# A hybrid decoder step on one core: sample values as one matmul per page on four column groups, and all convolution blocks as fused taps on VectorE

## What is computed

```python
u = glu_a * jax.nn.sigmoid(glu_g)
c, conv_new = causal_dwconv(u, conv_prev, conv_w, conv_b)      # 31 taps, 512 channels
...                                                            # LayerNorm over channels, SiLU -> a_out
z = jnp.einsum('bqhd,bkhd->bhqk', q, k) * (SB_HEAD_DIM ** -0.5) + bias
lb = jnp.where(mask, jax.nn.log_sigmoid(-z), 0.0)
rev = lax.cumsum(lb, axis=3, reverse=True)                     # 'after' is rev without its own key
wgt = jnp.where(mask, jnp.exp(jax.nn.log_sigmoid(z) + after), 0.0)
o = jnp.einsum('bhqk,bkhd->bqhd', wgt, v)
mixed = jnp.concatenate([a_out, o], axis=-1)
return mixed @ w_out, ...
```

## Time and profile before

| | us |
|---|---|
| median of 3 runs | 2577.05 (2575.78 to 2579.82) |
| the profiled execution | 2576.77 |
| its span in the trace | 2575.0 |
| VectorE busy in the span | 1362.9 (53%) |
| TensorE busy in the span | 2396.8 (93%) |
| GpSimd busy in the span | 426.9 (17%) |
| head loop, first to last subtraction of L1350 | 580.25 to 739.27 |
| output projection resumes | 772.58 |

### The profile page before, as it was taken

One profiled execution on the slowest core, in us unless ns is written; L12 is line 12 of the kernel. 1 busy time (PEld: TensorE's weight loads), 2 busy tenths in 40 slices (PEclk: granted clock), 3 DMA queues, 4 the chain that ended last, 5 costly groups with the idle time before them and its releaser, 6 DMA issues.

```text
span 2575.0 us, 45894 instructions
## 1 busy us (share of the span) xinstructions
PE 2396.8 (93%) x19221; PEld 2296.1 (89%) x19221; DVE 1362.9 (53%) x1492; ACT 826.5 (32%) x1025; POOL 426.9 (17%) x326
## 2 busy tenths in 40 slices
PE   7999999977989999999999998988889777999998
PEld 7999999864669999999999998878788767999997
DVE  4443444777834443445443444777676767443343
ACT  4221223134422221223221223352535343222223
POOL 0000012863303000003000002051423255000000
PEclk8999999977999999999999998989989898999999
DMA  4323226552422323223323323233232322333322
GB/s 134 92 80 106 81 82 179 172 167 81 141 65 66 88 79 110 82 74 107 98 81 99 98 68 102 67 97 88 74 94 83 103 62 78 85 86 102 98 74 75
DMA packets 409612, 244.48 MB, mean 95 GB/s; under 512 B 11363, under 2 KB 386475, under 8 KB 409441
## 3 DMA queue, kind: packets, MB, share of 16 engines
q1 hardware_dynamic: 409047, 242.61, 33.3%
q10 hardware_dynamic: 444, 0.17, 0.0%
HBM read 228.81 MB, written 14.58 MB: 95 GB/s over the span
## 4 chain that ended last, share of the span: by engine, by line
PE 76%; DVE 12%; ACT 5%; POOL 4%; issue 2%; DMA 0%; SPq 0%; ACTq 0%; POOLq 0%; DVEq 0%
PE PS L220 67%; POOL prod L872 3%; PE PS L1076 2%; DVE xcs L2028 2%; DVE cbuf L1251 1%; PE PS L959 1%; DVE wl L197 1%; PE PS L1810 1%; PE PS L1038 1%; DVE xcs L2195 1%; ACT wh L193 1%; DVE cdec L2206 1%; PE PS L1020 1%; PE PS L1727 1%; PE PS L969 1%
## 5 line engine op out<-in xcount | busy, mean ns | idle before, releaser
L220 PE MATMUL PS<-hh,wh 128*128 128x260 f32 x3792 | 776.5, 286 | 26.5 <-DVEq L637 7.6
L220 PE MATMUL PS<-hh,wl 128*128 128x260 f32 x3792 | 769.5, 285 | 0.0
L220 PE MATMUL PS<-hl,wh 128*128 128x260 f32 x3792 | 768.9, 285 | 0.0
L220 PEld LDWEIGHTS PS<-hh,wh 128*128 128x128 f32 x3792 | 590.6, 190 | 39.1 <-issue 22.5
L220 PEld LDWEIGHTS PS<-hh,wl 128*128 128x128 f32 x3792 | 589.2, 190 | 0.4
L220 PEld LDWEIGHTS PS<-hl,wh 128*128 128x128 f32 x3792 | 588.8, 190 | 0.4
L197 DVE TENSOR_TENSOR wl<-raw,wh 128x2048 fp32r<-128x2048 f32 (+2 forms) x194 | 442.7, 2282 | 205.3 <-ACT wh L193 204.8
L193 ACT ACTIVATE wh<-raw 128x2048 fp32r<-128x2048 f32 (+2 forms) x194 | 352.7, 1818 | 319.4 <-PE PS L220 283.9
L220 PE MATMUL PS<-hid_l,wh 128*128 128x260 f32 x1408 | 283.8, 283 | 0.0
L220 PE MATMUL PS<-hid_h,wh 128*128 128x260 f32 x1408 | 283.2, 282 | 0.0
L220 PE MATMUL PS<-hid_h,wl 128*128 128x260 f32 x1408 | 283.0, 282 | 0.0
(11 more groups left out here) (302 smaller groups left out, 2545.2 us busy)
## 6 DMA issues: line engine op xcount, KB each, us to landing
raw<-in_ffn_gate_dram SPq DMA_DIRECT2D x88, 512.0 KB, 4.0
raw<-in_ffn_up_dram SPq DMA_DIRECT2D x88, 512.0 KB, 5.2
raw<-in_ffn_down_dram SPq DMA_DIRECT2D x64, 384.0 KB, 4.1
raw<-in_ffn_down_dram SPq DMA_DIRECT2D x64, 320.0 KB, 3.6
raw<-in_m_in_proj_dram SPq DMA_DIRECT2D x40, 512.0 KB, 5.3
page<-in_cache_sb_v_dram SPq DMA_DIRECT2D x48, 256.0 KB, 2.7
raw<-in_ab_in_proj_dram SPq DMA_DIRECT2D x20, 512.0 KB, 5.3
ms_b<-in_state_ssm_dram SPq DMA_DIRECT2D x32, 256.0 KB, 3.0
```

Of the source, the lines that this page charges most:

```text
L220: ins = pe.matmul(out, x[:, k0, c:c + m], y[:, k, half * H2:(half + 1) * H2], start=k == 0 and a == 0, stop=k == nk - 1 and a == 2)
```

## The change

Three things are changed, all in `stage_a`.

1. **All four blocks on VectorE.** `tap`, GpSimd's additions and their semaphores go. `conv` runs over 124 taps instead of 93, 16 in a turn instead of 12.
2. **A page is one matmul.** The weights of all eight heads (8 columns of `dz`) stand in the array and the page's 512 columns stream past; the result is 8 rows by 512 columns, of which head h's row is wanted in its own 64 columns alone. Pages are taken in a new order (`value_page`): four samples at once, page pg of each, sample j of the four to the column group from row 32*j. `VROUNDS` becomes groups of four, at parts 1, 5 and 8 of turns 3, 4, 6, 7 and at parts 1 and 5 of turns 5 and 8; none is left in turn 9.
3. **The rows leave another way.** After four samples ScalarE copies the whole bank (`rows_out`, 128x512, twice in all) into `qb`, and at the end sixteen small matmuls against columns of `ident` pick each head's row out and turn it. The DMAs to `qrow` go. Bank 7 is zeroed once by VectorE (`orow_zero`), since these matmuls read all 128 rows; the first pages wait for it.

```diff
@@ on all engines
+                VQ = 4
+                two, three = ([0, VQ, 0, 0, 0, VQ, 0, 0, last] for last in (0, VQ))
+                VROUNDS = [0] * 3 * NR + (three * 2 + two) * 2 + [0] * NR
-                VROUNDS = [0] * 3 * NR + ([1] * (NR - 1) + [2]) * 6 + [1, 1, 0, 0, 0, 0, 0, 1, 1]
+                def value_page(v):
+                    g, r = divmod(v, VQ * NPG)
+                    pg, j = divmod(r, VQ)
+                    return g, pg, j
@@ on_sp
-                        load_page("cache_sb_v", i, vplace[i % NV], val_in[i % NV])
+                        g, pg, j = value_page(i)
+                        load_page("cache_sb_v", (g * VQ + j) * NPG + pg, vplace[i % NV], val_in[i % NV])
...
-                    for b in range(B):
-                        q = 32 * (b % 3)
-                        sp.wait_ge(S["orow_cp"], b + 1)
-                        sp.dma_start(qrow[b:b + 1, :], orow[b // 3][q:q + 1, :]).then_inc(S["orow_in"], 16)
@@ on_pool
-                    acc = cbuf[:, LC, 0:T]
-                    for w in range(1, CW):
...
-                        pool.tensor_tensor(acc, acc, prod[:, w % 2, :], ALU.add).then_inc(S["tap_add"], 1)
@@ on_pe, values()
+                            pe.wait_ge(S["orow_zero"], 1)
-                            if pg == 0 and b >= 3:
-                                pe.wait_ge(S["orow_cp"], b - 2)
-                            for h in range(NH):
-                                ins = pe.matmul(PS[q:q + 1, 7, h * DH:(h + 1) * DH], dz[:, b, pg, h:h + 1],
-                                                vplace[v % NV][:, h * DH:(h + 1) * DH], start=pg == 0 and h == 0,
-                                                stop=pg == NPG - 1 and h == NH - 1)
-                            ins.then_inc(S["dpv_mm"], 1)
+                            if pg == 0 and j == 0 and g >= 1:
+                                pe.wait_ge(S["orow_cp"], g)
+                            pe.matmul(PS[32 * j:32 * j + NH, 7, :], dz[:, g * VQ + j, pg, :], vplace[v % NV],
+                                      start=pg == 0, stop=pg == NPG - 1).then_inc(S["dpv_mm"], 1)
@@ on_pe, after the loop
-                    pe.wait_ge(S["orow_in"], 16 * B)
-                    for j in range(NB):
-                        ins = pe.transpose(PS[:, 5, j * B:(j + 1) * B], qrow[:, j * P:(j + 1) * P], ident[0:B, 0:B])
+                    pe.wait_ge(S["orow_cp"], B // VQ)
+                    for g in range(B // VQ):
+                        for h in range(NH):
+                            r, c = DH * (h % 2), h // 2 * B + g * VQ
+                            ins = pe.matmul(PS[r:r + DH, 5, c:c + VQ], qb[:, g, h * DH:(h + 1) * DH],
+                                            ident[:, h:P:P // VQ], start=True, stop=True)
@@ on_act
-                            tap(5)
...
-                        act.activation(orow[b // 3][q:q + 1, :], PS[q:q + 1, 7, :], ACT.Copy).then_inc(S["orow_cp"], 1)
+                        act.wait_ge(S["dpv_mm"], (g + 1) * VQ * NPG)
+                        act.activation(qb[:, g, :], PS[:, 7, :], ACT.Copy).then_inc(S["orow_cp"], 1)
@@ on_dve
-                        conv(12)
+                        conv(16)
+                            dve.wait_ge(S["dt_done"], 1)
+                            dve.memset(PS[:, 7, :], 0.0).then_inc(S["orow_zero"], 1)
```

More of the change, by code:

```diff
@@ L762, in stage_a @@
                 names = ("conv_in small_in masks tr_done cp_done u_done u0_mm u0_free u1_free gate_sig d_chain "
-                         "ln_cc ln_sq ln_ms ln_var ln_sd ln_cn ln_act ln_hi conv_done tap_done tap_add "
+                         "ln_cc ln_sq ln_ms ln_var ln_sd ln_cn ln_act ln_hi conv_done "
                          "qrow_tr qrow_cp qb_mm qb_cp key_in0 key_in1 v_tr v_cp misc_tr misc_cp row_cp kv_out "
@@ L766, in stage_a @@
                          "sp_done sum_mm t_done w_exp w_mask pv_mm pv_hi pv_lo dscore dabs de dlnp dsf_done dsum_mm "
-                         "dt_done dw_exp dpv_mm orow_cp orow_in os_tr os_hi mix_lo").split()
+                         "dt_done dw_exp dpv_mm orow_cp orow_zero os_tr os_hi mix_lo").split()
                 S = {n: nc.alloc_semaphore("a_" + n) for n in names}
@@ L951, in values @@
                             pe.wait_ge(S["dw_exp"], 1)
+                            pe.wait_ge(S["orow_zero"], 1)
                         for v in range(vstart(i, part), vstart(i, part + 1)):
[L953 to L954 removed]
+                            g, pg, j = value_page(v)
                             pe.wait_ge(val_in[v % NV], 16 * (v // NV + 1))
[L956 to L962 removed]
+                            if pg == 0 and j == 0 and g >= 1:
+                                pe.wait_ge(S["orow_cp"], g)
+                            pe.matmul(PS[32 * j:32 * j + NH, 7, :], dz[:, g * VQ + j, pg, :], vplace[v % NV],
+                                      start=pg == 0, stop=pg == NPG - 1).then_inc(S["dpv_mm"], 1)
                     def scores(h):
@@ L1131, in on_act, with rows_out @@
                     act.wait_ge(S["prod_done"], B * NPG)
[L1133 to L1141, removed]
-                            src, col = uA[:, LC, w:w + T], w * CB + LC
-                            if w == 0:
-                                act.activation(cbuf[:, LC, 0:T], src, ACT.Identity, scale=cwv[:, col:col + 1],
-                                               bias=vec[:, V_CB + LC:V_CB + LC + 1]).then_inc(S["tap_done"], 1)
-                                continue
-                            if w == 1:
-                                act.wait_ge(S["prod_free"], B * NPG)
-                            if w >= 3:
-                                act.wait_ge(S["tap_add"], w - 2)
-                            act.activation(prod[:, w % 2, :], src, ACT.Copy, scale=cwv[:, col:col + 1])\
-                                .then_inc(S["tap_done"], 1)
-                    def row_out(b):
-                        act.wait_ge(S["dpv_mm"], (b + 1) * NPG)
-                        q = 32 * (b % 3)
-                        act.activation(orow[b // 3][q:q + 1, :], PS[q:q + 1, 7, :], ACT.Copy).then_inc(S["orow_cp"], 1)
+                    def rows_out(g):
+                        act.wait_ge(S["dpv_mm"], (g + 1) * VQ * NPG)
+                        act.activation(qb[:, g, :], PS[:, 7, :], ACT.Copy).then_inc(S["orow_cp"], 1)
                     def front(h):
@@ L1199, in on_act @@
                             act.activation(fl(dsp), fl(dsp), ACT.Ln, bias=1.0).then_inc(S["dlnp"], 1)
-                        if i == 0:
-                            tap(2)
                         if 1 <= i <= NH:
@@ L1212, in on_act @@
                             hi_static(act, N0 + KS + 1)
-                        for b in range(B):
-                            if vstart(i - 1) < (b + 1) * NPG <= vstart(i):
-                                row_out(b)
+                        for g in range(B // VQ):
+                            if vstart(i) < (g + 1) * VQ * NPG <= vstart(i + 1):
+                                rows_out(g)
                         if i == NH:
@@ L1221, in on_act @@
                                 act.activation(lnsq(k), cbuf[:, k, :], ACT.Square).then_inc(S["ln_sq"], 1)
-                    row_out(B - 1)
                     act.wait_ge(S["os_tr"], 1)
@@ L1265, in conv @@
                         for _ in range(n):
-                            if pos[0] == LC * CW:
+                            if pos[0] == CB * CW:
                                 return
@@ L1388, in on_dve @@
                         if i == NH - 1:
-                            conv(LC * CW)
+                            conv(CB * CW)
                             dve.sem_inc(S["conv_done"], 1)
```

6 lines of the change are left out of this document (removed).

## The result

The changed kernel took 2549.68 us, median of 4 runs (2548.73 to 2551.12), beside 2577.30 for the kernel before: a ratio of 0.9895, 95% interval 0.9882 to 0.9907. In a later comparison, on another chip, it was 2548.61 and 0.9893 (0.9876 to 0.9909). The forecast was 2553, with a range of 2545 to 2569. The profiled execution took 2551.12 with a span of 2549.4, 25.65 less than that of before, 2576.77.

A forecast was written before the change was run, and what follows sets the result against it. VectorE's taps, slowed by GpSimd, bound turns 4 to 5, TensorE's one-by-one pages bound the loop from turn 6. The projection resuming 28.7 us earlier, less 5 for the clock, takes 23.7 off 2576.77: 2553, range 2545 to 2569.

The forecast's parts named there:

- s1, s2: Starts of VectorE's subtraction (L1350) in turns 1 and 2 of the head loop, predicted at 582.1 and 603.7.
- s3, s4, s5, s6: Starts of VectorE's subtraction in turns 3 to 6, predicted at 628.6, 647.6, 668.0 and 687.0; the last was 697.12.
- s7, s8: Starts of VectorE's subtraction in turns 7 and 8, predicted at 703.1 and 719.2; the latter was 739.27.
- Taps: VectorE in the head loop: 31 more taps, 124 in all; with GpSimd idle 0.78 us each, 12.55 for 16.
- Pages: TensorE in the head loop: four pages on four column groups overlap almost fully, taken as 1.1 us a group.
- rival 1: TensorE's pages: groups overlap only by half, 2.45 us a group, turns 7 and 8 lose 2.7 each; 2558.5, chance 0.15.
- Turns 7 and 8: Head loop, bound by TensorE: 16.1 us each, with 7.96 for the head's own matmuls and 2.2 for two groups.
- The end: Behind the last subtraction: 10.9 us on TensorE instead of 17.0, then 1.2 for sixteen small matmuls replacing four transposes.
- The clock: TensorE in the head loop: idle gaps make turns open at the lower clock, costing 5 us in all, bounds 2 to 12.
- rival 2: TensorE's pages: no overlap, 3.9 us a group, 19.7 lost together over turns 3 to 8, no clock loss; 2568, chance 0.11.
- 3: Page transfers: pages arrive late, a turn's third group 2 to 3 us late in five turns; 2563, chance 0.07.
- 4: TensorE in the head loop: clock stays low throughout, a turn takes 27.8 us, the kernel gets slower; 2610, chance 0.07.

The follow-up runs named there:

- one_group: The changed kernel with four consecutive pages going to the same column group instead of to four; 2567.40 us, 0.9954 of the kernel before.

## Why the prediction was right, point by point

Times of the changed kernel, less the 1.7 by which its stage started late, beside the prediction's steps without clock loss:

| | predicted | measured |
|---|---|---|
| s1, s2 | 582.1, 603.7 | 582.1, 603.1 |
| dz subtraction, memset | 615.0, 0.6 | 613.8, 0.48 |
| s3, s4, s5, s6 | 628.6, 647.6, 668.0, 687.0 | 627.4, 646.4, 666.8, 685.8 |
| s7, s8 | 703.1, 719.2 | 702.5, 719.6 |
| small matmuls end | 731.3 | 731.2 |
| projection resumes | 743.9 | 743.7 |

- **Taps** (0.78 each, turns 1 to 6 VectorE's): right, 12.55 for 16, and shown by two experiments to be GpSimd's doing. Two small gains I had not counted put s3 to s6 1.2 earlier: without additions beside it the subtraction's successor (L1357, now L1327) took 1.49 in turn 2 instead of 2.09; and the wait for the sample scores' sum was 4.79 instead of 5.36, because the last matmul of that sum ran at a granted clock of 0.75 instead of 0.50 (1.34 for 1.92). The second is luck: with the additions on scratch, none of which run by then, the wait was 5.36 again.
- **Pages** (1.1 a group): right in kind, 0.97 from a group to the next matmul. The rule of the Trainium skill ("TensorE: Matmul & The Clock Gate", Part 3) that packed matmuls start and end in program order, by which the time would have been rival 1's, does not hold here for the starts: a page is one call in the program, so its second pass stands ahead of the next page's first, yet at 622.52 to 622.97 all four first passes start ahead of the second ones. The sentence at the top that each engine works through its instructions in order is too strong for these passes.
- **Turns 7 and 8** (16.1 each): 16.66 and 17.13, and without the clock's share 15.2 and 15.7. The 7.96 for the head's own matmuls was too high: it was taken from a turn in which pages stood between them, and together they take 7.1 (3.75 less 1.38, 3.88 and 0.86 in turn 8). In turn 8 I forgot the subtraction at 710.03, 0.68, which stands ahead of the values.
- **The end** (10.9 and 1.2 for the small matmuls): 10.5 and 1.06.
- **The clock** (5, bounds 2 to 12): the mechanism right, the term mis-sized and partly misplaced. In the stage it cost 2.8: 1.43 of waiting in turn 7, and 1.38 in the values of turn 8 (3.75 for 2.37). The zero-weight matmuls gave turn 8's part back; turn 7's is read from the rows alone. Turns 3 to 6 hid all of theirs. Another 1.5 came in the rest, where the prediction had nothing: the projection opens at 0.70 instead of 0.83, with 59 matmuls for 68 in its first 10 us and 668 for 678 in its first 90. At 85 in 10 us, the full rate, ten are 1.2 us, which is what the fifth weight split shows. The last 0.3 come some 1100 us later, and no run shows that they are the clock's.

So the terms without the clock were 2.9 too cautious (28.8 and 2.8 measured, 28.7 forecast), and the clock cost 4.3 at most for 5: 27.3 off by the stage and the rest, against 23.7 forecast. Between the medians the gain is 27.6, and the forecast lies 3.3 above what was measured.

**The rivals.** 1 and 2 fell by the group's 1.04, and one_group is rival 2 made real. 3 fell: pages waited for a DMA, but for 0.48 at 648.04 and 0.17 at 705.42, in pieces where TensorE waits anyway. 4 fell: in turns 3 to 8 every sum opens at the upper level, its first two passes in 1.12 to 1.13, and over the whole sums of turns 7 and 8 the granted clock was 1.00; it was back by the end of the values and pages ahead of them.

## What to carry to other kernels

Before work is shared between VectorE and GpSimd, price the instruction on VectorE beside the other's: where both read two tensors from SBUF, an addition given away can cost more than it saves (here 0.9 us for 0.75). Matmuls with few output rows belong on different column groups and next to each other, where four cost little more than one (here 1.04 us, and 1.02 for the single page at 705.42). And when a change takes work from TensorE, count what the lower clock costs in the turns that nothing hides and in the stream behind the stage, and deal the freed engine's work into the turns that now idle.

## What the runs showed of the hardware that I had not expected

- Four fp32 matmuls of 512 columns on four column groups take 1.04 us, on two 1.89, on one 3.60, and their passes start out of program order.
- GpSimd's additions and VectorE's two-input instructions slow each other with no data in common: tap 0.75 to 1.67, addition 1.26 at its fastest to 1.66 on average. The Trainium skill ("SBUF — State Buffer", SBUF: two separate sides) calls the port pair that they share an exclusive lock, on which the later instruction waits for the whole of the earlier. The direction agrees; the size is less: a tap and an addition in turn would be 0.75 + 1.26 = 2.01, an estimate by that rule, and a tap beside an addition took 1.67.
- The clock of a stream can differ with what ran in the turns ahead of it. The projection opened at 0.70 in the changed kernel and at 0.79 with zero-weight matmuls, though TensorE waited 6.0 us just ahead of it in both; the rest was 1814.2 and 1814.0 against 1812.7 and 1812.5, alike within 0.2 in both profiles of each. What decides the level there is not shown.
